# Third stage's sample updates in another order, first unit of the fourth stage split and run there, second stage's norms between value units

## What is computed

```python
def gla_chunk(S, inp):                 # mixer B, 4 heads, state 128 x 256 each
    q, k, v, lg = inp
    Bc = jnp.cumsum(lg, axis=-2)
    D = jnp.exp(jnp.where(incl[..., None], Bc[..., :, None, :] - Bc[..., None, :, :], -jnp.inf))
    A = jnp.einsum('bhtc,bhjc,bhtjc->bhtj', q, k, D)
    o = jnp.einsum('bhtc,bhcv->bhtv', q * jnp.exp(Bc), S) + jnp.einsum('bhtj,bhjv->bhtv', A, v)
    S_new = S * jnp.swapaxes(jnp.exp(BL), -1, -2) + jnp.einsum('bhjc,bhjv->bhcv', k * jnp.exp(BL - Bc), v)
    return S_new, o
...
o_a, S_a_new = run_chunked(gdn_chunk, ...)                                  # mixer A, 8 heads
o_a = rmsnorm(o_a, norm_a) * jax.nn.silu(z); y_a = o_a @ w_proj_a
o_b = rmsnorm(o_b, norm_b) * jax.nn.silu(r_b); y_b = o_b @ w_proj_b
out = (sigmoid(g_a) * y_a + sigmoid(g_b) * y_b) @ w_out
```

## Time and profile before

| | us |
|---|---|
| median of 3 runs (lowest to highest) | 930.96 (925.15 to 933.14) |
| profiled execution | 929.58 |
| its span | 927.9 |
| TensorE busy in the span | 860.5 (93%) |
| VectorE, ScalarE, GpSimd busy | 410.2, 303.3, 212.3 |

### The profile page before, as it was taken

The page is one execution under the profiler, slowest core; times in us unless marked ns, Lnnn a source line. Parts: engine busy times, 40 slices in busy tenths (PEclk is TensorE's granted clock), DMA queues, the critical chain, the costliest instruction groups (busy, mean ns, idle before and its releaser), DMA issues. The chain is left out here.

```text
span 927.9 us, 16207 instructions
## 1 busy us (share of the span) xinstructions
PE 860.5 (93%) x6828; PEld 715.9 (77%) x6828; DVE 410.2 (44%) x691; ACT 303.3 (33%) x604; POOL 212.3 (23%) x241
## 2 busy tenths in 40 slices
PE   8999988989799989999789999997999999999984
PEld 6988877989777979675589999996996565666451
DVE  4688874545433432155666331662352222222223
ACT  6685464232142135232564444333101100110003
POOL 8511307474300110000553005656000000000000
PEclk7999999999865799999699999999989999999998
DMA  8933107000001369502745454441478999999991
GB/s 232 300 119 112 43 1 197 1 1 1 1 8 46 91 206 321 181 6 91 237 141 167 152 171 148 166 152 46 140 320 369 422 420 420 421 420 420 420 399 58
DMA packets 98021, 175.51 MB, mean 189 GB/s; under 512 B 9076, under 2 KB 84436, under 8 KB 85605
## 3 DMA queue, kind: packets, MB, share of 16 engines
q1 hardware_dynamic: 97944, 174.42, 52.3%
HBM read 163.13 MB, written 10.95 MB: 188 GB/s over the span
## 5 line engine op out<-in xcount | busy, mean ns | idle before, releaser
L276 PE MATMUL ps<-rounded,rounded 128*128 128x304 f32 x632 | 200.5, 317 | 5.6 <-ACT arena L1790 2.8
L278 PE MATMUL ps<-rounded,rounded 128*128 128x304 f32 x632 | 195.4, 309 | 0.0
L277 PE MATMUL ps<-hL,rounded 128*128 128x304 f32 x504 | 156.6, 311 | 0.0
L276 PEld LDWEIGHTS ps<-rounded,rounded 128*128 128x128 f32 x632 | 123.4, 195 | 17.6 <-issue 12.3
L278 PEld LDWEIGHTS ps<-rounded,rounded 128*128 128x128 f32 x632 | 123.4, 195 | 0.0
L264 DVE TENSOR_TENSOR rounded<-ring,rounded 128x2048 fp32r<-128x2048 f32 x33 | 76.9, 2331 | 58.7 <-ACT rounded L258 58.3
L264 POOL TENSOR_TENSOR rounded<-ring,rounded 128x2048 fp32r<-128x2048 f32 x15 | 68.8, 4590 | 146.8 <-ACT rounded L258 146.6
L277 PEld LDWEIGHTS ps<-hL,rounded 128*128 128x128 f32 x504 | 99.6, 198 | 0.4 <-issue 0.2
L258 ACT ACTIVATE rounded<-ring 128x2048 fp32r<-128x2048 f32 x48 | 91.4, 1910 | 19.1 <-PE ps L278 16.2
L1130 PE MATMUL ps<-arena 128*128 128x128 f32 (+1 forms) x576 | 64.7, 277 | 1.6 <-DVE arena L1035 1.1
L1130 PEld LDWEIGHTS ps<-arena 128*128 128x128 f32 (+1 forms) x576 | 62.2, 192 | 3.2 <-DVE arena L1035 1.9
(11 more groups left out here) (404 smaller groups left out, 1564.3 us busy)
## 6 DMA issues: line engine op xcount, KB each, us to landing
ring<-in_w_in SPq DMA_DIRECT2D x36, 1024.0 KB, 7.2
ring<-in_expert_w_gate SPq DMA_DIRECT2D x16, 1024.0 KB, 20.9
ring<-in_expert_w_up SPq DMA_DIRECT2D x16, 1024.0 KB, 16.0
ring<-in_expert_w_down SPq DMA_DIRECT2D x16, 1024.0 KB, 24.0
arena<-in_expert_w_down SPq DMA_DIRECT2D x12, 1024.0 KB, 21.2
arena<-in_expert_w_gate SPq DMA_DIRECT2D x12, 1024.0 KB, 21.6
arena<-in_expert_w_up SPq DMA_DIRECT2D x12, 1024.0 KB, 24.4
ring<-in_w_proj_a SPq DMA_DIRECT2D x4, 1024.0 KB, 4.8
```

Source lines behind the costliest of these rows:

```text
L276: self.nc.tensor.matmul(self.psum[b][:, 0:NT], h[:, j, c], xh(j), start=(j == 0), stop=False)
L277: self.nc.tensor.matmul(self.psum[b][:, 0:NT], h[:, j, c], xl(j), start=False, stop=False)
L278: ins = self.nc.tensor.matmul(self.psum[b][:, 0:NT], lo[:, j, c], xh(j), start=False, stop=(j == KB - 1))
```

## The change

Three things are moved; no arithmetic is added or dropped.

1. The norms of mixer A (squares, sums, roots, scalings of 8 heads) move from the start of `merge` into `gla`, one head behind each of the value units 2 to 9. All eight sums use bank 7. The copies of sample rows on SP wait for them, since they share memory.
2. The tail of `gla` is reordered: updates 1 stands between queries 1 and 2, updates 2 in front of the outputs, and VectorE's update of the prompt state stands behind the third head.
3. Slot `N_Z` is split in the tail of `gla` (high part on ScalarE behind the four copies to `OLD`, low part on GpSimd), and its two blocks run there, one in front of updates 3 and one behind it. `OLD` moves, as the high part `FIRST_Z` lies where it was. `merge` keeps the four norms of mixer B, with unit 2 between sums 1 and 2, and unit 3 behind them.

```diff
@@ class Core
+        self.FIRST_Z = self.carve_r(8480, SW)
@@ gla
+    SQ, RS = ([k.carve(18816 + 608 * n + NT * p, NT) for p in range(2)] for n in range(2))
-    OLD = [k.carve(at, 512) for at in (10112, 10624, 11392, 11904)]
+    OLD = [k.carve(at, 512) for at in (10528, 11040, 11552, 22400)]
@@ gla, SP
         sp.wait_ge(s["kd_ready"], 3)
+        sp.wait_ge(s["on_ready"], HA)
@@ gla, GpSimd
+        for h in range(HA):
+            if h >= 2:
+                pl.wait_ge(s["sum_done"], h - 1)
+            nc.gpsimd.tensor_tensor(SQ[h % 2], oaT[:, h, :], oaT[:, h, :], ALU.mult).then_inc(s["sq_ready"], 1)
+        pl.wait_ge(s["sq_ready"], HA)
...
+        k.low_part(pl, nc.gpsimd, N_Z, HI, k.FIRST_Z)
@@ gla, ScalarE
             if u == 2:
                 k.high_part(act, N_Z - 1, HI)
+            if 2 <= u < 10:
+                h = u - 2
+                act.wait_ge(s["sum_done"], h + 1)
+                if h >= 2:
+                    act.wait_ge(s["on_ready"], h - 1)
+                link(nc.scalar.activation(RS[h % 2], psum[7][:, 0:NT], ACT.Ln, scale=1 / 128, bias=k.epsc))
+                nc.scalar.activation(RS[h % 2], RS[h % 2], ACT.Exp, scale=-0.5).then_inc(s["rs_ready"], 1)
...
+        act.wait_ge(s["s_ready"], SC2)
+        k.high_part(act, N_Z, HI, k.FIRST_Z)
@@ gla, VectorE
         k.low_part(dve, nc.vector, N_Z - 1, HI)
+        for h in range(HA):
+            dve.wait_ge(s["rs_ready"], h + 1)
+            nc.vector.scalar_tensor_tensor(oaT[:, h, :], oaT[:, h, :], k.na, RS[h % 2], ALU.mult, ALU.mult).then_inc(s["on_ready"], 1)
...
-            if h == 1:
+            if h == 2:
@@ gla, TensorE
             ins.then_inc(unit_done, 1)
+            if 2 <= u < 10:
+                h = u - 2
+                pe.wait_ge(s["sq_ready"], h + 1)
+                if h:
+                    pe.wait_ge(s["rs_ready"], h)
+                mm(psum[7][:, 0:NT], k.ones[:, :], SQ[h % 2], start=True, stop=True).then_inc(s["sum_done"], 1)
...
         updates(0)
+        for h in range(2):
+            old_queries(h)
         updates(1)
+        for h in range(2, HB):
+            old_queries(h)
+        updates(2)
...
-        updates(2)
+        k.block_of_slot(pe, N_Z, 0, 0, [k.FIRST_Z] * 3)
         updates(3)
+        pe.wait_ge(s["s_ready"], SC3)
+        k.block_of_slot(pe, N_Z, 1, 4, [k.FIRST_Z] * 3)
@@ merge, ScalarE
-        for n in range(N_Z, N_Z + 3):
-            k.high_part(act, n, HI)
+        k.high_part(act, N_Z + 1, HI)
         act.wait_ge(k.stored, STORED_GLA)
-        for h in range(12):
+        for h in range(HB):
...
+            if h == 1:
+                k.high_part(act, N_Z + 2, HI)
@@ merge, VectorE
-        for n in range(N_Z, N_Z + 3):
-            k.low_part(dve, nc.vector, n, HI)
-        for h in range(12):
+        k.low_part(dve, nc.vector, N_Z + 1, HI)
+        for h in range(HB):
...
+            if h == 1:
+                k.low_part(dve, nc.vector, N_Z + 2, HI)
@@ merge, TensorE
+        square_sum(0)
+        square_sum(1)
+        k.block_of_slot(pe, N_Z + 1, 0, 2, HI)
+        square_sum(2)
+        square_sum(3)
+        for u in range(3, 4):
+            k.block_of_slot(pe, N_Z + u // 2, u % 2, u, HI)
         for u in range(4, 48):
+            if u == 5:
+                pe.wait_ge(s["rs_ready"], HB)
```

More of the change, by code:

```diff
@@ L1327, in gla @@
     ident, U, SL, SL3, U3, R03, GR = k.ident, k.U, k.SL, k.SL3, k.U3, k.R03, k.GR
-    PLACE, hH, hL, psum, bank4, unit_done, lrT = k.PLACE, k.hH, k.hL, k.psum, k.bank4, k.unit_done, k.lrT
+    PLACE, hH, hL, psum, bank4, unit_done, lrT, oaT = k.PLACE, k.hH, k.hL, k.psum, k.bank4, k.unit_done, k.lrT, k.oaT
     QK = k.carve(0, 8 * NT, 8, NT)
@@ L1394, in _ @@
         nc.gpsimd.tensor_copy(AT2[64:64 + l3, :, :], bc_mid(ident[64:64 + l3, 64:64 + l3], HB)).then_inc(s["pad_ready"], 1)
+        pl.wait_ge(s["pad_ready"], 3)
+        k.low_part(pl, nc.gpsimd, N_Z, HI, k.FIRST_Z)
     def out(act, i):
@@ L1549, in _ @@
                 for g in range(HB):
[L1550 removed]
+                    nc.vector.scalar_tensor_tensor(S[:, g, :], S[:, g, :], EX2[:, g, 0, TAIL - 1:TAIL], psum[(1, 4)[g // 2]][:, 256 * (g % 2):256 * (g % 2) + 256],
                                                    ALU.mult, ALU.add).then_inc(s["s_ready"], 1)
@@ L1581, in _ @@
             l = L[c]
+            if c == 1:
+                pe.wait_ge(s["rs_ready"], HA)
             if c == 2:
@@ L1676, in _, with old_queries @@
         updates(0)
-        for h in range(HB):
+        def old_queries(h):
             pe.wait_ge(s["old_ready"], h + 1)
@@ L1707, in merge @@
     nc, i_, o_ = k.nc, k.i_, k.o_
-    oaT, ones, psum, unit_done, epsc, na, nb = k.oaT, k.ones, k.psum, k.unit_done, k.epsc, k.na, k.nb
+    oaT, ones, psum, unit_done, epsc, nb = k.oaT, k.ones, k.psum, k.unit_done, k.epsc, k.nb
     obT = k.carve(0, 8 * NT, 8, NT)
@@ L1734, in merge @@
     base = units(N_Z)
+    SB = (5, 6, 7, 1)
     def ob(v, j):
@@ L1755, in _ @@
     def _(pl):
-        for h in range(12):
+        for h in range(HB):
             if h >= 2:
                 pl.wait_ge(s["sum_done"], h - 1)
-            if h < 8:
-                nc.gpsimd.tensor_tensor(SQ[h % 2][:, 0, :], oaT[:, h, :], oaT[:, h, :], ALU.mult).then_inc(s["sq_ready"], 1)
-            else:
-                v = obT[:, h - 8::4, :]
-                nc.gpsimd.tensor_tensor(SQ[h % 2][:, :, :], v, v, ALU.mult).then_inc(s["sq_ready"], 1)
+            v = obT[:, h::4, :]
+            nc.gpsimd.tensor_tensor(SQ[h % 2][:, :, :], v, v, ALU.mult).then_inc(s["sq_ready"], 1)
         for j in range(8):
@@ L1789, in _ @@
                 act.wait_ge(s["gated"], u - 1)
-            nc.scalar.activation(ZT[:, u % 2, :], psum[u % 4][:, 0:NT], ACT.Silu).then_inc(s["silu_ready"], 1)
+            nc.scalar.activation(ZT[:, u % 2, :], psum[4 if u == 1 else u % 4][:, 0:NT], ACT.Silu).then_inc(s["silu_ready"], 1)
             if u % 2:
@@ L1822, in _ @@
     def _(dve):
-        for n in range(N_Z, N_Z + 3):
-            k.low_part(dve, nc.vector, n, HI)
-        for h in range(12):
+        k.low_part(dve, nc.vector, N_Z + 1, HI)
+        for h in range(HB):
             dve.wait_ge(s["rs_ready"], h + 1)
-            if h < 8:
-                nc.vector.scalar_tensor_tensor(oaT[:, h, :], oaT[:, h, :], na, RS[:, h % 2, :], ALU.mult, ALU.mult).then_inc(s["on_ready"], 1)
-            else:
-                for e in range(2):
-                    v = obT[:, h - 8 + 4 * e, :]
-                    nc.vector.scalar_tensor_tensor(v, v, nb[:, e:e + 1], RS[:, h % 2, :], ALU.mult, ALU.mult).then_inc(s["on_ready"], 1)
-        dve.wait_ge(s["on_ready"], 16)
+            for e in range(2):
+                v = obT[:, h + 4 * e, :]
+                nc.vector.scalar_tensor_tensor(v, v, nb[:, e:e + 1], RS[:, h % 2, :], ALU.mult, ALU.mult).then_inc(s["on_ready"], 1)
+            if h == 1:
+                k.low_part(dve, nc.vector, N_Z + 2, HI)
+        dve.wait_ge(s["on_ready"], 2 * HB)
         for u in range(16):
@@ L1898, in _, with square_sum @@
         mm = nc.tensor.matmul
-        for h in range(12):
+        def square_sum(h):
             pe.wait_ge(s["sq_ready"], h + 1)
-            if h >= 4:
-                pe.wait_ge(s["rs_ready"], h - 3)
-            if h < 8:
-                ins = mm(psum[4 + h % 4][:, 0:NT], ones[:, :], SQ[h % 2][:, 0, :], start=True, stop=True)
-            else:
-                mm(psum[4 + h % 4][:, 0:NT], ones[:, :], SQ[h % 2][:, 0, :], start=True, stop=False)
-                ins = mm(psum[4 + h % 4][:, 0:NT], ones[:, :], SQ[h % 2][:, 1, :], start=False, stop=True)
-            ins.then_inc(s["sum_done"], 1)
-            if h in (3, 5, 7, 9):
-                u = (h - 3) // 2
-                k.block_of_slot(pe, N_Z + u // 2, u % 2, u, HI)
+            for e in range(2):
+                ins = mm(psum[SB[h]][:, 0:NT], ones[:, :], SQ[h % 2][:, e, :], start=(e == 0), stop=(e == 1))
+            ins.then_inc(s["sum_done"], 1)
+        square_sum(0)
[5 more added lines that the diff above has]
+            k.block_of_slot(pe, N_Z + u // 2, u % 2, u, HI)
         for u in range(4, 48):
+            if u == 5:
+                pe.wait_ge(s["rs_ready"], HB)
             if u - 4 < 16:
```

9 lines of the change are left out of this document (4 added, 5 removed).

## The result

| | before | after |
|---|---|---|
| median of 20 runs each (lowest to highest), us | 927.58 (921.35 to 935.53) | 922.06 (913.96 to 930.50) |
| profiled execution, its span | 929.58, 927.9 | 921.91, 920.2 |

The ratio is 0.9934, 95% interval 0.9906 to 0.9962: 6.1 us less, between 3.5 and 8.7. It is estimated from the runs in the fast state, so it isn't the quotient of the two medians, which lie 5.5 us apart. The kernel after is faster, but by less than the 1% that the forecast of 918 promised. The sum had said -12.2.

The account below looks back on a forecast made before the run. TensorE, 93% busy, was taken to bound the kernel, with holes from the third stage's tail to unit 4. +5.25 - 0.3 - 17.2 = -12.2 gave 917.3 from the profiled 929.58, 918.7 from the 930.96 median, stated as 918; range 914.5 to 925.

Parts of the forecast that it names:

- Step 1: Value units: the norms moved there add 5.25 us, eight sums plus one 1.15 wait; bounds 4.1 and 6.4.
- The rival in which the units lose their clock: Value units: the bank 7 wait drops the clock, nine units cost 25 us more, 942; chance of slower 0.04.
- Step 2: Tail of the third stage: two blocks go in, yet the stage ends 0.3 us earlier.
- The replay of the order: Tail: the new order timed with the old trace's durations; VectorE ends at 445.15 against 445.60 before.
- I take full clock, as TensorE no longer waits here: Tail blocks: assumes 2.4 GHz; at 1.2 GHz block 0 would cost up to 2.7 us more.
- the clock's rival: Tail falls to low clock: 2.7 for block 0, 0.9 for block 2; 8.6 saved, 922; chance 0.20.
- Step 3: Head of the fourth stage, release to unit 4: 17.2 us shorter, 32.5 to 15.3; bounds 16.3 and 18.0.
- the bound of 1.3: Fourth stage start: GpSimd's third square coming before VectorE's low part would cost up to 1.3 us.
- The wait for the stores: Fourth stage start: stores must land before ScalarE's first root, at 4.4 us, without effect.
- The rival without a gain at the end: From 680 on: a weight stream starting at its own time sets the end, which stays 930; chance 0.06.
- The chance of 0.68: Whole kernel: faster by more than 1% (9.3 us), from the forecast and a little of the low-clock tail case.

Follow-up runs that it names:

- run 6: Kernel after with ScalarE's weight copy behind head 0's root and VectorE's low part behind its norm: ratio 0.9925 to the kernel before.
- run 7: Kernel after with block 0 woven among outputs and state products, head 0's root ahead of the weight copy, fillers in two fourth-stage pauses: ratio 0.9867 to before.
- runs 8 and 9: One program, twice: run 7 with ScalarE's weight copy ahead of its table load, fillers 9 and 5; ratios 0.9856 and 0.9823 to the kernel before.
- run 4: Kernel after with 9 and 15 unread dense matmuls in TensorE's two pauses at the fourth stage's start: ratio 0.9903 to the kernel before.

## Why the prediction was right in direction and wrong in size

The forecast's steps, in its order; with the two unedited segments (+0.5 and +1.4) they make up the distance from -12.2 to -5.8.

**Step 1 held** (+5.34 for +5.25): eight sums of 0.51, which make 4.08 (run 6 has just that over before), and 1.26 for the one wait (1.03 of it idle in the trace) for the 1.15 that ScalarE's queue gave. The rival in which the units lose their clock is out: 1.00 over the stretch.

**Step 2 is the step that failed** (+2.94 for -0.3). The replay of the order was right to 0.2 (26.3 without the loss, for 26.4). The term that was wrong is the line "I take full clock, as TensorE no longer waits here": the clock fell without a wait, behind outputs and state products, for 3.4 us. The forecast had the row that spoke against it. In the kernel before, TensorE worked on to 437.2, and its clock had gone earlier: 0.67 over two microseconds is full clock to 436.7 and half from there.

```profile
434.00:436.00 2.00, 2.00 (x17) 1.73 (x17) 1.56 (x4) 0.49 (x1) 0.00 (x0) 1.00 0.00 0
436.00:438.00 2.00, 1.23 (x17) 0.59 (x9) 1.73 (x5) 0.00 (x0) 0.00 (x0) 0.67 0.79 272
```

The rival named this ("it fell right behind the narrow output matmuls") and gave it 0.20, with 922 as its time. The argument against it, that TensorE had stood waiting, does not cover the half microsecond before the wait. That rival is what happened, with another split: it priced block 0 at 2.7 and measured is 1.5 there and 2.0 in the state products ahead of it. The Trainium skill (TensorE: Matmul & The Clock Gate, What's actually happening), which the rival cited for a gate that runs freely of the kernel's start, would let the same code meet either level; runs 7 to 9 agree (the same tail at 1.00 throughout, and with 1.7 and 3.4 lost, the last on another chip), the four traces of the tail as changed don't need it.

**Step 3 was short by 1.1** (-16.1 for -17.2), from two terms. Block 2 was priced at 4.2, between 3.34 and 5.06; it took 4.96, as the clock fell at 456.6, among the first sums and behind the pause of 2.41, and with a second pause of 1.33 it stayed down to 463.4; run 4, with fillers in both pauses, gave it back. And block 2 began 0.3 later, 6.05 after the release, since VectorE's low part ended late. VectorE, then GpSimd, at this place:

```profile
457.25 2.76 DVE L265 TENSOR_TENSOR rounded<-ring,rounded 128x2048 fp32r<-128x2048 f32 x1 [4.67 <-ACT rounded L259]
...
462.66 2.28 DVE L265 TENSOR_TENSOR rounded<-ring,rounded 128x2048 fp32r<-128x2048 f32 x1
```

```profile
456.66 1.20 POOL L1800 TENSOR_TENSOR arena<-arena 128x608 f32<-128x608 f32 x1 [0.27 <-PE ps L1939]
458.81 2.25 POOL L1800 TENSOR_TENSOR arena<-arena 128x608 f32<-128x608 f32 x1 [0.95 <-PE ps L1939]
```

The low part takes 2.28 alone and 2.76 here, because the third square was already running until 457.86; the fourth square then took 2.25 instead of 1.20. The forecast had the third square 0.2 behind the low part, as it had doubled all of the first sums; those of head 0 ran at full clock (the fall came at 456.6) and the order turned. The Trainium skill (SBUF — State Buffer, Who interferes with whom) says that whichever of the two issues first keeps the other waiting: the trace agrees in both directions. The price was 0.5, not the bound of 1.3. The wait for the stores, put at 4.4, ended at 4.46 after the release and cost nothing:

```profile
454.01 1.28 ACT L1813 ACT_TABLE_LOAD   x1 [13.84 <-PEq L1735]
...
458.47 0.51 ACT L1820 ACTIVATE arena<-ps,small 128x304 f32<-128x304 f32 x1 [1.25 <-DMA out_sg_p<-arena]
```

From the second pair of sums to unit 4 it took 5.37 for 5.35.

**Behind unit 4** the gain arrived but for 1.4: that segment takes 199.2 to 201.1 over the fourteen traces, none of which edits it, so this is scatter. SP's queue and the end bear it out, 248.79 behind this row as 248.72 before (248.7 to 253.1 over the fourteen):

```profile
671.41 2.00 SPq L238 DMA_DIRECT2D arena<-in_expert_w_down  x4
```

The rival without a gain at the end is out. The range, 914.5 to 925, held because the clock's rival was priced into it, and with some luck: it stood on a median of three runs, 930.96, where twenty give 927.58. Counted from there it would be 911.1 to 921.6, which 922.06 just misses, and the rival's 922 would be 919: its saving was 8.6, the measured one 6.1. The chance of 0.68 for more than 1% was too high, since that rival deserved more than 0.20.

**A version that beats both**: runs 8 and 9, by 1.4 and 1.8% against the kernel before, from six executions each (intervals above). They were not timed side by side with the kernel after, whose ratio is 0.9934; by the segments they are 5.0 and 3.9 us ahead of it. Of its edits, the head-0 order (1.26) and the start of the fourth stage (1.5 and 1.5) are shown by their segments in more than one trace; the weaving is not shown to gain (all 118.6, 119.7 and 118.9 with it, 119.4 without).

## What to carry to other kernels

When work is moved behind a run of narrow matmuls, price it at the low clock if any trace shows the clock going down near that kind of work, even when the engine will be busy throughout: read the granted clock microsecond by microsecond up to the first 0.50, and look at what ran before it, not only at the wait behind it. Dense work among the narrow may only delay the fall and costs its own time, so it has to be tried. And a stretch with pauses of one or two microseconds can lose the clock too, though it needn't (four of five traces here); filling such pauses is cheap (24 fillers brought 1.5, and with fillers no trace of six lost the clock there).

## What the runs showed that was not expected

- TensorE's clock fell to 1.2 GHz with the engine busy 1.00 of every microsecond (439.5 in the kernel after). In all thirteen traces whose tail lost the clock, before among them, it fell within the tail, 15 to 23 us after the first state query; in one it didn't. What in the narrow work lets it fall (few rows, few columns, or their share) was not separated and stays open.
- One program lost 1.7 and 3.4 us in the same tail in two executions (runs 8 and 9), on two chips, while the tail as changed lost 3.4 in four traces at one place.
- Three full-width matmuls behind every narrow group cost 1.4 us over the same work in one piece (run 7, one trace), at full clock and with TensorE busy throughout; why is not shown.
